# Gates made earlier in a two-layer PEER kernel, and four more places for its dense weight units

## The chip, the cores and the metric

One core of one Trainium2 chip runs the whole program in one launch. The metric is device time in microseconds (us). Three timed runs of the kernel before gave 2160.9, 2161.8 and 2163.95 us; the median is 2161.8 us. The profile is of one more execution.

## The reference, cut to what matters

256 tokens of 1024 features pass through two transformer layers (retention, then differential attention) and a third block (gated linear attention, MLA, cross attention, feed-forward). After each of the first two mixers stands a PEER feed-forward, and only it is touched by the change:

```python
def block(xc):                                    # 128 tokens
    q = (xc @ w_q).reshape(PEER_CHUNK, PEER_HEADS, 2, half)
    sc = jnp.einsum('thpd,hpnd->thpn', q, subkeys)            # 8 heads x 2 x 128 keys
    s1, i1 = lax.top_k(sc[:, :, 0], 16); s2, i2 = lax.top_k(sc[:, :, 1], 16)
    cand = s1[..., :, None] + s2[..., None, :]
    top, pos = lax.top_k(cand, 16)                            # 16 experts per head
    gate = jax.nn.softmax(top, axis=-1)
    u_e, v_e = jnp.take(u, idx, axis=0), jnp.take(v, idx, axis=0)   # of 16384 experts
    act = jax.nn.gelu(jnp.einsum('ted,td->te', u_e, xc))
    return jnp.einsum('te,ted->td', gate * act, v_e)
x = layer_norm(ALPHA * x + peer_ffn(x), g, b)
```

All of it is in float32.

## The kernel before, in words

The kernel splits the 256 tokens of each PEER layer in two.

**Dense tokens.** For the last 160 tokens (DENSE) all 16384 experts are computed. Both tables, u and v, are read once each as 128 units of 128 experts (512 KB per unit), by SyncE, in order, into N_PLAIN = 6 places (`plain`, in the room of the hi and lo weight splits, which idle in this stage). Unit i waits until TensorE has used unit i - 6. In the u stage TensorE takes two units per step c (c = 0 to 63, j = 0, 1), eight matmuls each (16 instructions in the profile), and ScalarE applies gelu. In the v stage (`second_weights`) it takes unit k = 0 to 127 against the gated activations `experts`. At k = 122 (128 - LATE) it waits until all looked-up experts are used (L1020), and after k = 127 turns the sums back to token order (`turn_back`).

**Looked-up tokens.** The first 96 tokens (LOOKED) use only their own 16 x 8 experts. With 128 partitions this makes 96 gathers (LISTS) of 128 rows of u, and 96 of v: q = 0 to 191, 512 KB each. GpSimd issues them (`look_up`, L3179) into six places (N_ROWS): gather q waits until VectorE has used row set q - 6. VectorE uses each in `look(q)` (L2495 for u, L2501 for v), at points of its own order of work that `peer_schedule` lays out: LOOKS_AT[c, j] in the u stage, LOOKS_AT[k] in the v stage. 90 looks fall in the u stage and 102 in the v stage.

**Gates.** VectorE finds the experts (`topk`) in pieces of YIELDS = 15 instructions between these points; they run out at c = 11. The softmax is ScalarE's Exp (before step c = LISTED = 20), VectorE's `gates` at c = 20 and TensorE's `turn` of three columns after the units of c = 20 (L819), then VectorE's `turned_gates` at c = 21. 20 looks stand ahead of `gates` on VectorE. On GpSimd (`beside_experts`) stand, in order: `early` = 26 gathers, four small DMAs of the lists, a wait for the gates, six small DMAs of the gates and a wait for their landing, then the builds. Before build i all gathers up to GATHERS[i] are issued: 29 before the first.

**Spread.** From step c = SPREAD = 22 on, the gates are placed into `experts` for four dense tokens at a time, 40 groups. GpSimd (L3168, two instructions), ScalarE and VectorE build one-hot rows for a group, TensorE multiplies them (`spread`, L967), ScalarE and VectorE place the result. There is one group for each c, and TensorE does spread(i - 1) where the others build i; its first is at c = 23, after the first unit.

**Later work in GpSimd's queue.** Between the gathers of q = 126 and 127 stands `later()`. In layer 0 it waits until TensorE has used v unit k = 48 and loads constants (L3253); in layer 1 it waits for k = 54 and loads the memory tokens and eight constants (L3272). In layer 1 VectorE and ScalarE also have steps of the third block between their looks (`remember`): at k = 72 to 84 angles and the norm of the memory tokens (L2740), which TensorE transposes at k = 90 and 92 (L819).

**End of a layer.** VectorE copies two of four v sums (`turned_back`, L2543), TensorE turns them, and VectorE adds them to x (L2184), takes statistics (L2189) and normalizes (`norm_steps`).

## Time and profile before

| | us |
|---|---|
| median of three runs | 2161.8 |
| profiled execution | 2162.51 |
| its span | 2160.6 |
| TensorE busy in it | 2011.0 |
| VectorE busy | 1384.3 |
| GpSimd busy | 659.0 |
| mean DMA rate over the span | 283 GB/s |

The profiled execution is 1.9 us longer than its span. A busy TensorE is not one at its peak: matmuls are pipelined. A stretch of the views is given in us from the start of the span, and "xN" counts instructions.

### The profile page before, as it was taken

How to read it: one execution, taken by the hardware profiler on the slowest of the kernel's cores; microseconds unless marked ns; L12 is line 12 of the kernel's file. 1: busy time of each engine (PE TensorE's matmuls, PEld its weight loads, DVE VectorE, ACT ScalarE, POOL GpSimd, SP SyncE). 2: the span in 40 equal slices, each digit the busy share in tenths (PEclk: the TensorE clock that was granted, in tenths of full speed). 3: DMA queues.
4: the chain of work that ended last, by engine and by line, in shares of the span. 5: the costliest groups of instructions: out<-in, count | busy, mean ns of one | idle time of the engine just before them, and what ended most of it. 6: DMA issues, size and time to landing. Idle time of an engine off the chain costs nothing.

```text
span 2160.6 us, 32850 instructions
## 1 busy us (share of the span) xinstructions
PE 2011.0 (93%) x13084; PEld 1842.1 (85%) x13084; DVE 1384.3 (64%) x2732; ACT 599.7 (28%) x1179; POOL 659.0 (31%) x631
## 2 busy tenths in 40 slices
PE   9999995899999998989999499999999499999999
PEld 9877995899998987867799499999998488777887
DVE  7567499677744344358759957774314725877885
ACT  3455411232200000026530023320000203665554
POOL 1000013888842333000101478884133510000000
PEclk9999998999999999989999799999999799999999
DMA  7546588999999999824558899999999993343665
GB/s 262 176 149 204 183 255 328 351 393 395 386 409 389 356 409 409 312 80 136 165 196 289 304 351 394 390 389 408 370 343 409 362 349 119 108 147 113 189 193 167
DMA packets 168952, 612.42 MB, mean 283 GB/s; under 512 B 19600, under 2 KB 19776, under 8 KB 168544
## 3 DMA queue, kind: packets, MB, share of 16 engines
q1 hardware_dynamic: 107712, 391.63, 50.4%
q0 software_dynamic: 60368, 217.38, 26.5%
q8 instruction: 105, 1.72, 0.3%
q10 hardware_dynamic: 720, 1.31, 0.2%
q14 instruction: 47, 0.39, 0.1%
HBM read 606.89 MB, written 1.05 MB: 281 GB/s over the span
## 4 chain that ended last, share of the span: by engine, by line
PE 64%; DMA 18%; DVE 14%; ACT 1%; issue 1%; POOL 1%; ACTq 0%; DVEq 0%; POOLq 0%
PE ps L981 18%; PE ps L1012 12%; DMA plain<-in_peer_v 12%; PE ps L684 5%; DMA big<-in_peer_v,big 4%; PE ps L720 4%; PE ps L723 4%; PE ps L727 3%; PE ps L767 3%; PE ps L687 3%; DVE big L2328 2%; PE ps L967 2%; DVE big L2096 2%; DVE big L2324 2%; PE ps L819 1%; PE ps L756 1%
## 5 line engine op out<-in xcount | busy, mean ns | idle before, releaser
L1012 PE MATMUL ps<-big,plain 128*128 128x160 f32 x4096 | 600.0, 305 | 29.5 <-DMA plain<-in_peer_v 20.3
L1012 PEld LDWEIGHTS ps<-big,plain 128*128 128x128 f32 x4096 | 568.1, 192 | 61.7 <-DMA plain<-in_peer_v 33.0
L981 PE MATMUL ps<-big,plain 128*128 128x160 f32 x4096 | 580.5, 302 | 1.0 <-DMA plain<-in_peer_u 0.8
L981 PEld LDWEIGHTS ps<-big,plain 128*128 128x128 f32 x4096 | 563.9, 191 | 1.9 <-issue 1.0
L2501 DVE SCALAR_TENSOR_TENSOR big<-big 128x1024 f32<-128x1024 f32 x188 | 241.5, 1284 | 311.6 <-DMA big<-in_peer_v,big 309.1
L2090 DVE TENSOR_TENSOR lo<-raw,hi 128x1024 fp32r<-128x1024 f32 (+1 forms) x195 | 236.2, 1219 | 102.8 <-ACT hi L1491 102.3
L3179 POOL DMA_INDIRECT big<-in_peer_v,big x192 | 192.1, 1001 | 278.4 <-DVE big L2501 255.1
L3179 POOL DMA_INDIRECT big<-in_peer_ur,big x192 | 221.2, 1152 | 145.6 <-DVE big L2495 91.6
L2495 DVE CUSTOM_DVE_ANT_0 big<-big 128x1024 f32<-128x1024 f32 x192 | 241.7, 1269 | 10.4 <-DMA big<-in_peer_ur,big 10.2
L1491 ACT ACTIVATE hi<-raw 128x1024 fp32r<-128x1024 f32 (+1 forms) x195 | 204.7, 1055 | 148.5 <-PE ps L727 53.0
L3168 POOL TENSOR_SCALAR lnp<-iota,selT 128x128 f32<-128x128 f32 x160 | 193.2, 1213 | 3.2
L1674 ACT ACTIVATE big<-ps 128x320 f32<-128x320 f32 (+39 forms) x126 | 44.4, 354 | 480.5 <-PE ps L981 453.9
L684 PE MATMUL ps<-xs,hi 128*128 128x512 f32 x512 | 128.8, 393 | 1.0 <-DVE big L3087 1.0
L819 PE MATMUL ps<-ident,big 128*128 128x128 f32 (+1 forms) x280 | 42.4, 285 | 86.0 <-DVE big L2462 54.4
L819 PEld LDWEIGHTS ps<-ident,big 128*128 128x128 f32 (+1 forms) x280 | 33.9, 144 | 95.6 <-DVE big L2462 55.4
L2441 DVE SCALAR_TENSOR_TENSOR big<-ps,big 128x192 f32<-128x192 f32 (+19 forms) x80 | 41.7, 521 | 109.2 <-ACT big L1666 88.1
L684 PEld LDWEIGHTS ps<-xs,hi 128*128 128x128 f32 x512 | 92.2, 189 | 17.8 <-DVE big L3087 1.1
L720 PE MATMUL ps<-hi,xs 128*128 128x512 f32 (+1 forms) x308 | 99.1, 403 | 1.9 <-ACT xs L1566 1.7
L723 PE MATMUL ps<-hi,xs 128*128 128x512 f32 (+1 forms) x308 | 95.7, 392 | 0.2 <-DVE xs L2216 0.2
L727 PE MATMUL ps<-lo,xs 128*128 128x512 f32 (+1 forms) x308 | 94.8, 389 | 0.5 <-DVE lo L2090 0.5
L1497 ACT ACTIVATE big<-ps 128x512 f32<-128x512 f32 (+6 forms) x121 | 64.8, 547 | 72.1 <-PE ps L727 46.7
L1491 ACT ACTIVATE tail_weights<-raw 128x1024 fp32r<-128x1024 f32 x3 | 3.2, 1058 | 270.5 <-PE ps L1012 270.5
(402 smaller groups left out, 2301.1 us busy)
## 6 DMA issues: line engine op xcount, KB each, us to landing
plain<-in_peer_u SPq DMA_DIRECT2D x256, 512.0 KB
plain<-in_peer_v SPq DMA_DIRECT2D x256, 512.0 KB
raw<-in_ret_vg SPq DMA_DIRECT2D x32, 512.0 KB
raw<-in_peer_q SPq DMA_DIRECT2D x24, 512.0 KB
raw<-in_ffn_up SPq DMA_DIRECT2D x22, 512.0 KB
raw<-in_ffn_down SPq DMA_DIRECT2D x22, 512.0 KB
raw<-in_ffn_gate SPq DMA_DIRECT2D x18, 512.0 KB
raw<-in_ret_qk SPq DMA_DIRECT2D x16, 512.0 KB
```

The lines of the kernel that those rows point to most:

```text
L684: e.matmul(out, uh[:, k, :], xs[:, k, :, :].rearrange("p h t -> p (h t)"), start=k == 0, stop=False)
L720: e.matmul(out, xh[:, 2 * s + i, cut], uh[:, i, :], start=s == 0 and i == 0, stop=False)
L723: e.matmul(out, xl[:, 2 * s + i, cut], uh[:, i, :], start=False, stop=False)
L727: ins = e.matmul(out, xh[:, 2 * s + i, cut], ul[:, i, :], start=False, stop=s == 3 and i == 1)
L981: ins = e.matmul(u.view[:, j * DENSE:(j + 1) * DENSE], w[:, k, :], Peer.xT[:, k, :], start=k == 0, stop=k == 7)
L1012: ins = e.matmul(us[b // 2].view[:, b % 2 * DENSE:(b % 2 + 1) * DENSE], w[:, b * 128:(b + 1) * 128], experts[:, k, :], start=k == 0 and b ...
L1491: e.activation(parts(i)[0][:, 0:w], raw[:, i % N_RAW, 0:w], ACT.Copy).then_inc(s_hi, 1)
L2090: e.tensor_tensor(ul[:, 0:w], raw[:, i % N_RAW, 0:w], uh[:, 0:w].bitcast(F32), ALU.subtract).then_inc(s_lo, 1)
L2495: e.tensor_tensor_reduce(rows, rows, copies, 1.0, 0.0, ALU.mult, ALU.add, w).then_inc(s_looked, 1)
L2501: e.scalar_tensor_tensor(out=sums, in0=rows, scalar=w, in1=sums, op0=ALU.mult, op1=ALU.add).then_inc(s_looked, 1)
L3168: ins = e.tensor_scalar(Peer.oha[i % 2][:, t % 4, :], iota[:, :], selT[:, 0, t:t + 1], selT[:, 2, t:t + 1], ALU.is_equal, ALU.mult)
L3179: e.indirect_dma_start(out=Peer.rows[m % N_ROWS], out_offset=None, in_=table, in_offset=bass.IndirectOffsetOnAxis(ap=Peer.idx[:, i:i + 1], ...
```

## The change

The gates follow the selection more closely: `gates` moves from c = 20 to c = 14 (GATED), the wait and the turn on TensorE from c = 20 to c = 23 (LISTED), `turned_gates` from c = 21 to c = 22 (TURNED), the first group from c = 22 to c = 26 (SPREAD), and the 40 groups then come five in nine units in place of one in two. From c = 12 to c = 25 VectorE has one look per c in place of four in five units, so that 9 looks stand ahead of `gates`, 15 gathers ahead of the gates' DMAs and 27 ahead of the first build on GpSimd; 82 looks fall in the u stage and 110 in the v stage. `later()` moves from behind q = 126 to behind q = 145.

The dense units get ten places: the four new ones lie in `xs`, the room of the hi and lo activations. In layer 0 all ten are used throughout; in layer 1 units from i = 210 (k = 82) on use only the first six, since `xs` is written again at k = 90. The first loads into the new places wait for the last matmul of the query projection.

At the end of a layer VectorE adds and takes statistics of the first half of the columns before it copies the last v sums.

```diff
-N_PLAIN, N_ROWS, LATE = 6, 6, 6
-YIELDS, LISTED, SPREAD, LOOKS = 15, 20, 22, 8
+N_PLAIN, N_FIRST, N_ROWS, LATE = 10, 6, 6, 6
+SLOTS = [[i % 10 for i in range(256)], [i % 10 if i < 210 else (i - 210) % 6 for i in range(256)]]
+YIELDS, GATED, TURNED, LISTED, SPREAD, LOOKS = 15, 14, 22, 23, 26, 8
...
-            n = 1 if c >= SPREAD and (2 * (c - SPREAD) + j) % 2 == 0 else 0
+            n = 1 if c >= SPREAD and (2 * (c - SPREAD) + j) % 9 % 2 == 0 else 0
...
-            n = 1 if c >= LOOKS and (2 * (c - LOOKS) + j) % 5 < 4 and q < LISTS else 0
+            n = 1 if c >= LOOKS and q < LISTS and ((2 * (c - LOOKS) + j) % 5 < 4 if c < GATED - 2 or c >= SPREAD else j == 0) else 0
...
+    later = min(q for k in range(58, 128) for q in looks[k]) + N_ROWS
...
-        plain = nc.alloc_sbuf_tensor_at("plain", [128, N_PLAIN, UNIT], F32, offset=split_at)
+        plain_a = nc.alloc_sbuf_tensor_at("plain", [128, N_FIRST, UNIT], F32, offset=split_at)
...
+        plain_b = nc.alloc_sbuf_tensor_at("plain_in_xs", [128, N_PLAIN - N_FIRST, UNIT], F32, offset=xs_at)
+        plain = [plain_a[:, i, :] for i in range(N_FIRST)] + [plain_b[:, i, :] for i in range(N_PLAIN - N_FIRST)]
...
-                    if c == LISTED - 1:
+                    if c == LISTED - 2:
                         for t in range(2):
                             e.wait_ge(s_sel, 2 * l + t + 1)
                             e.activation(Peer.sel[t][2], Peer.sel[t][2], ACT.Exp).then_inc(s_gexp, 1)
...
-                        if (c, j) == (LISTED, 0):
+                        if (c, j) == (GATED, 0):
                             gates()
-                        if (c, j) == (LISTED + 1, 0):
+                        if (c, j) == (TURNED, 0):
                             turned_gates()
...
-                for i in (0, 2):
-                    turned_back(l, i)
+                turned_back(l, 0)
+                for t in range(2):
+                    residual(f"peer_v{l}", t, 0)
+                for t in range(2):
+                    stats(f"peer_v{l}", t, 0)
+                turned_back(l, 2)
...
-                early = N_ROWS + sum(len(LOOKS_AT[c, j]) for c in range(LISTED) for j in range(2))
+                early = N_ROWS + sum(len(LOOKS_AT[c, j]) for c in range(GATED) for j in range(2))
...
-                    if q == LISTS + 30:
+                    if q == LATER:
                         later()
...
             def plain_load(l, i):
                 if i < N_PLAIN:
-                    e.wait_ge(s_used, split_before[m] + 1)
+                    e.wait_ge(s_used, split_before[l, i] + 1)
                 else:
-                    e.wait_ge(*plain_used(l, i - N_PLAIN + 1))
+                    e.wait_ge(*plain_used(l, max(n for n in range(i) if SLOTS[l][n] == SLOTS[l][i]) + 1))
```

`residual` is the addition to x (L2184) and `stats` the statistics (L2189) of one half, cut out of `norm_steps`, which leaves out the first half for these two stages.

## Rows read from the trace of the kernel before

**Rows 1.** The page's busy times, whole span: engine, us, share, instructions.
```profile
PE 2011.0 (93%) x13084; PEld 1842.1 (85%) x13084; DVE 1384.3 (64%) x2732; ACT 599.7 (28%) x1179; POOL 659.0 (31%) x631
```

**Rows 2.** Waits of TensorE, 240 to 960: us in total, times, longest.
```profile
PE ps L819 <- DVE big L2462: 26.9, 1, 26.9
PE ps L819 <- DVE x L2201: 4.0, 1, 4.0
```

**Rows 3.** Waits of TensorE, 1100 to 1830.
```profile
PE ps L819 <- DVE big L2740: 29.2, 1, 29.2
PE ps L819 <- DVE big L2462: 27.5, 1, 27.5
```

**Rows 4.** Windows: length, busy us of PE, PEld, DVE, ACT, POOL; PEclk; DMA share; GB/s.
```profile
630.00:675.00 45.00, 42.94 (x283) 38.59 (x282) 22.23 (x18) 0.00 (x0) 16.81 (x18) 1.00 1.03 409
680.00:712.00 32.00, 31.53 (x225) 30.57 (x226) 6.42 (x5) 0.00 (x0) 0.00 (x0) 1.00 0.91 320
1125.00:1150.00 25.00, 25.00 (x186) 25.00 (x186) 24.80 (x168) 2.62 (x6) 0.00 (x0) 1.00 0.75 244
1540.00:1590.00 50.00, 49.49 (x361) 48.76 (x360) 4.70 (x4) 0.00 (x0) 6.89 (x11) 1.00 0.88 296
```

**Rows 5.** Timeline of VectorE, 360 to 383: start, us, what [idle before <-releaser].
```profile
360.29 1.22 DVE L2495 CUSTOM_DVE_ANT_0 big<-big 128x1024 f32<-128x1024 f32 x1
369.77 1.22 DVE L2495 CUSTOM_DVE_ANT_0 big<-big 128x1024 f32<-128x1024 f32 x1 [1.38 <-DMA big<-in_peer_ur,big]
380.87 0.28 DVE L2107 TENSOR_REDUCE sm<-big 128x8 f32<-128x128 f32 x1
382.18 0.29 DVE L2462 TENSOR_TENSOR big<-big,sm 128x128 f32<-128x128 f32 x1
```

**Rows 6.** Timeline of TensorE at the gates' turn and the first group, layer 0.
```profile
381.77 1.66 PE L819 MATMUL ps<-ident,big 128*128 128x128 f32 x6 [26.87 <-DVE big L2462]
398.36 0.62 PE L967 MATMUL ps<-lnp 128*128 128x128 f16 x8 [2.23 <-issue]
```

**Rows 7.** Timeline of GpSimd, 363 to 417, layer 0.
```profile
363.77 1.99 POOL L3179 DMA_INDIRECT big<-in_peer_ur,big  x1 [0.30 <-issue]
366.06 1.99 POOL L3179 DMA_INDIRECT big<-in_peer_ur,big  x1 [0.30 <-issue]
383.00 2.08 POOL L3193 DMA_DIRECT2D big<-big  x4
392.27 1.83 POOL L3179 DMA_INDIRECT big<-in_peer_ur,big  x1 [4.20 <-issue]
396.67 1.59 POOL L3168 TENSOR_SCALAR lnp<-iota,selT 128x128 f32<-128x128 f32 x2
413.10 3.90 POOL L3168 TENSOR_SCALAR lnp<-iota,selT 128x128 f32<-128x128 f32 x2
```

**Rows 8.** Groups on GpSimd, 405 to 585: busy us, mean ns, idle before.
```profile
L3168 POOL TENSOR_SCALAR lnp<-iota,selT 128x128 f32<-128x128 f32 x76 | 94.9, 1254 | 1.5
L3179 POOL DMA_INDIRECT big<-in_peer_ur,big x59 | 68.3, 1157 | 17.0 <-issue 12.1 <-DVE big L2495 4.9
```

**Rows 9.** Timeline of GpSimd at `later()`, layers 0 and 1.
```profile
712.45 0.58 POOL L3253 DMA_DIRECT2D big<-in_c_diff_cs  x1 [34.85 <-PE ps L1012]
1581.48 0.77 POOL L3272 DMA_DIRECT2D big<-in_mem  x1 [47.10 <-PE ps L1012]
```

**Rows 10.** Timeline of VectorE and TensorE, v stage of layer 0: start, last look, k = 122.
```profile
595.06 28.44 PE L1012 MATMUL ps<-big,plain 128*128 128x160 f32 x208
887.98 1.28 DVE L2501 SCALAR_TENSOR_TENSOR big<-big 128x1024 f32<-128x1024 f32 x1 [1.28 <-DMA big<-in_peer_v,big]
900.73 3.60 PE L1024 MATMUL ps<-big,selT 128*128 128x512 f32 x8
```

**Rows 11.** v stage of layer 1: its start in the chain, k = 122 in the timeline.
```profile
1452.12 34.93 PE ps L1012 x256
1779.06 3.60 PE L1024 MATMUL ps<-big,selT 128*128 128x512 f32 x8
```

More of the change, by code:

```diff
@@ L240, in peer_schedule @@
     assert q == 2 * LISTS and last is not None
-    return steps, looks, tokens, gathers, last
-STEPS_AT, LOOKS_AT, TOKENS, GATHERS, ALL_LOOKED = peer_schedule()
+    later = min(q for k in range(58, 128) for q in looks[k]) + N_ROWS
+    return steps, looks, tokens, gathers, last, later
+STEPS_AT, LOOKS_AT, TOKENS, GATHERS, ALL_LOOKED, LATER = peer_schedule()
 def build(nc, A, OUT):
@@ L631, in build @@
             for i in range(N_PLAIN):
-                m = 256 * l + i
-                split_before[m] = max(n for n in in_ring[m % N_PLAIN % N_SPLIT] if n < end)
+                split_before[l, i] = max(n for n in in_ring[i % N_SPLIT] if n < end) if i < N_FIRST else end - 1
             for r in range(N_SPLIT):
                 n = min(n for n in in_ring[r] if n >= end)
-                m = max(m for m in range(256 * l, 256 * l + 256) if m % N_PLAIN % N_SPLIT == r)
-                W.after[n] = (*W.after.get(n, ()), (s_pused, m + 1))
+                i = max(i for i in range(256) if SLOTS[l][i] in (r, r + N_SPLIT))
+                W.after[n] = (*W.after.get(n, ()), (s_pused, 256 * l + i + 1))
         n = W.first["diff_k0"]
@@ L2176, in acc, with residual, stats @@
                         left(k + lead)
+            def residual(stage, t, h):
+                u, xp = use[stage, 2 * t + h], x[:, t, h * 512:(h + 1) * 512]
+                e.wait_ge(*u.filled)
+                e.scalar_tensor_tensor(out=xp, in0=xp, scalar=ALPHA, in1=u.view, op0=ALU.mult,
+                                       op1=ALU.add).then_inc(u.freed[0], 1)
+            def stats(stage, t, h):
+                e.wait_ge(*use[stage, 2 * t + h].freed)
+                me.did(e.bn_stats(st[:, (2 * t + h) * 6:(2 * t + h + 1) * 6], x[:, t, h * 512:(h + 1) * 512]))
             def norm_steps(i, stage, tiles=(0, 1)):
+                halves_left = (1,) if stage in ("peer_v0", "peer_v1") else (0, 1)
                 for t in tiles:
                     xt = x[:, t, :]
-                    for h in range(2):
-                        u, xp = use[stage, 2 * t + h], x[:, t, h * 512:(h + 1) * 512]
-                        e.wait_ge(*u.filled)
-                        e.scalar_tensor_tensor(out=xp, in0=xp, scalar=ALPHA, in1=u.view, op0=ALU.mult,
-                                               op1=ALU.add).then_inc(u.freed[0], 1)
+                    for h in halves_left:
+                        residual(stage, t, h)
                     yield
-                    for h in range(2):
-                        e.wait_ge(*use[stage, 2 * t + h].freed)
-                        me.did(e.bn_stats(st[:, (2 * t + h) * 6:(2 * t + h + 1) * 6], x[:, t, h * 512:(h + 1) * 512]))
+                    for h in halves_left:
+                        stats(stage, t, h)
                     me.wait()
```

22 lines of the change are left out of this document (11 added, 11 removed).

## The prediction

> **What bounds the kernel now.** I read the page's busy times, the waits of TensorE, windows of 25 us and shorter, and then the timelines of the engines in turn where TensorE stood still. TensorE is busy for 2011.0 of 2160.6 us [rows 1], so most of the kernel is paced by it. The reader is to see three other things.
>
> First, three long waits: 26.9 and 27.5 us for the gates at the turn (L819 for L2462), once a layer, and 29.2 us in layer 1 for the normed memory tokens (L2740) [rows 2, 3].
>
> Second, which bound holds between the waits. An undisturbed TensorE takes 186 instructions in 25 us, so a dense unit of 16 costs 25 x 16 / 186 = 2.15 us, and that needs 0.524 MB / 2.15 us = 244 GB/s [rows 4]. With gathers beside it the DMA engines stand at 409 GB/s, or 1.28 us for a transfer of 512 KB, and TensorE takes 283 instructions in 45 us: 2.54 us per unit, twice the 1.28 us. The two streams then share evenly; I count 2.56 us for a unit and 2.56 us for a gather, side by side. So the v stages are DMA-bound while gathers remain, and TensorE-bound afterwards.
>
> Third, the gathers stop in each v stage for `later()`, which waits 34.85 and 47.10 us for TensorE [rows 9]. In these stretches the DMA engines move 320 and 296 GB/s in place of 409 [rows 4]. In layer 1 the stop also delays VectorE's looks, and with them the memory tokens' norm that stands between them: the 29.2 us of [rows 3].
>
> **The gates (layer 0; layer 1 alike).** TensorE stops at 381.77 - 26.87 = 354.9 [rows 6] with the 42 units of c = 0 to 20 done. The change lets it go on to the end of c = 23, 6 x 2.15 = 12.9 us, until 367.8. The selection ends just before the look at 360.29 [rows 5], as now, since YIELDS is the same. Three looks of 1.22 us and the gates (380.87 to 382.47, 1.6 us) put the gates at 360.3 + 3.7 + 1.6 = 365.6, 2 us before TensorE asks. That wait goes.
>
> What is late next is the first group. GpSimd's fifteenth gather is the one at 366.06, done at 368.05 [rows 7]. Behind it stand the ten small DMAs and their landing, 383.00 to 392.27 = 9.3 us, so gathers resume at 377.3. Then 12 gathers precede the first build, where 3 do now, and the last of them waits for the look of the first six. Gather to look took 369.77 - 363.77 = 6.0 us [rows 5, 7]. So: first of the twelve landed at 383.5; two more at 2.56 us each beside the dense stream; then TensorE stands, the ten places fill, and three come at 1.28 us, the sixth by about 392.5. Look 1.2, the gather it releases 1.1, a build 1.6 [rows 7]: the first group's rows are there at 396.4, and TensorE can start at about 397. It asks at 367.8 + 1.7 for the turn + 7 units x 2.15 = 384.5. A wait of some 12.5 us takes the place of 26.9. Now the first group is at 398.36 with 47 units done [rows 6]; then it is at about 397 with 55. Gain 8 x 2.15 + 1.4 = 18.6 us. Bounds: no wait at the group, 26.9 + 2.2 = 29 us; all twelve spaced by 2.56 us and a look between, TensorE at 405, gain 17.2 - 6.6 = 10.6 us. I take 18.6, since the places do fill once TensorE stands.
>
> **The denser groups.** In nine units TensorE needs 9 x 2.15 + 5 x 0.56 = 22.2 us (the turn of a group is L967, 0.62 us with its start [rows 6]). GpSimd needs 5 builds of (94.9 + 1.5) / 38 = 2.54 us and 7.2 gathers of (68.3 + 12.1) / 59 = 1.36 us [rows 8]: 22.5 us. It becomes the bound by 0.3 us in nine units, 3 us over 76; now it has 4.5 x 2.54 + 9.8 = 21.2 us of work in 21.9 us. A u stage gains 18.6 - 3 = 15.6 us. ScalarE and VectorE have room (VectorE 64% busy over the span [rows 1]).
>
> The Trainium skill (SBUF — State Buffer, "Who interferes with whom") says that a VectorE instruction with two SBUF inputs blocks GpSimd instructions that read SBUF, fully. The trace shows build pairs from 1.59 to 3.90 us [rows 7]; what makes the slow ones no row here shows. If denser work on VectorE did this more often, that is the slower rival below.
>
> **The v stages.** Layer 0 runs from 595.06 to k = 122 at 900.73, its last look ends at 889.3 [rows 10]. Check of the two-stream count: 102 looks x 2.56 = 261 us, plus 35 us of stop, is 296; it took 294. TensorE gets 259 / 2.56 = 101 units in it, 35 / 2.15 = 16 more in the stop, less 3 raw weight units in the same queue: 114.5. It had in fact used 122 - 11.4 / 2.15 = 116.7 when the looks ended, so it entered the stage with a lead of 2.2 units.
>
> After the change 110 looks remain, 110 x 2.56 - 2 = 280 us, with no stop if `later()` comes after k = 48: at q = 145, 58 looks or 148 us into the stage, TensorE is at k = 58 or more, and needs 48 (54 in layer 1). Four more places are a lead of up to 4 more units, filled while DMA has room (244 of 409 GB/s before the gathers start [rows 4]). TensorE then has used 280 / 2.56 - 3 + 6.2 = 112.6 units when the looks end, and reaches k = 122 after 280 + 9.4 x 2.15 = 300 us, against 305.7. Gain 5.7 us in layer 0. If the four places give nothing, 8.6 us less.
>
> Layer 1 now takes 1779.06 - 1452.12 = 327 us [rows 11]. After the change the same 280 us apply, plus 11 us for the constants, 4.3 transfers of 512 KB in the gathers' half (now in the stop, where DMA has room). In 291 us TensorE uses 291 / 2.56 - 3 + 6.2 = 116.9 units, then 5.1 x 2.15: 302 us. Gain 25 us. The memory tokens stay a wait of perhaps 10 us at k = 90 and 92, since the look of k = 84 (the 84th in the stage) ends at 84 x 2.56 + 11 for the constants = 226 us, the norm is a few us behind it, and TensorE can be at k = 92 by (92 - 6) x 2.56 = 220. It is free: the transfers go on behind it, and TensorE catches up before the looks end. From k = 82 on six places do as well as ten, because the dense stream has none landed ahead of use.
>
> **The end of a layer.** One addition and one statistic of 512 columns (0.65 us each, by half of 1.28 us for a look's 1024 columns [rows 10]) leave the path behind the last sums; they move under the last 12 half units on TensorE. TensorE's 4.0 us for the norm [rows 2] shrink by 1.3 us in layer 0; in layer 1 other matmuls cover it. The same work costs 2.7 us if it delays the last copies; the last units cover it. The second tile's share is hidden. Everything else (another ring order behind the stage, first loads of the new places) I put at 0, within 1 us either way.
>
> **Sum.** Layer 0: 15.6 + 5.7 + 1.3 = 22.6. Layer 1: 15.6 + 25 = 40.6. Together 63 us. The profiled execution took 2162.5 us, 0.7 us above the median of the runs, so the forecast is 2162.5 - 63 = 2099 us.
>
> **The rivals.**
> - *No wait at the first group.* The gathers land before 384.5, and 12.5 us more are saved in each layer: 2099 - 25 = 2074 us. For it: a gather alone is issued each 1.25 us. Against it: 12 of them behind a resumption at 377.3 with a latency of 6 us.
> - *The four places give nothing.* The lead is spent before the v stage because GpSimd's gathers take the DMA share: 2 x 8.6 = 17 us less, 2116 us. For it: the lead of 2.2 units out of six places now. This is the case in which half of the change doesn't do what it says.
> - *TensorE still waits long for the memory tokens or the stop stays.* The 110 later looks outweigh the stop removed, and 20 to 24 of layer 1's 25 us are not won: 2122 us. For it: the norm stands behind the 84th look of the stage, and 8 more looks are in it. Against it: the stop of 47 us goes.
> - *GpSimd becomes the bound: slower.* A pair of builds took from 1.59 to 3.90 us [rows 7], mean 2.50. Were all 3.90 in the denser order, 40 groups x 1.4 = 56 us are lost per layer in the u stage, 2099 + 112 = 2211 us. It decides for slower once a group costs 5.3 us in place of 4.5 (63 / 80 = 0.8 us more). Against it: VectorE's work per group hardly changes, only its spacing by a tenth.
>
> **How the numbers follow.** Chances: forecast 0.54, no wait 0.12, places give nothing 0.20, memory wait 0.09, slower 0.05. The lower end is the second case, 2074. At the upper end I add to the forecast the bound of the first group (8 us per layer) and half of the places' worth: 2099 + 16 + 9 = 2124, which holds the two middling cases. 0.2% or 4.3 us is about what can be told from no change; hardly any case ends there. Faster 0.93, same 0.02, slower 0.05.
>
> **What would show it.** Right: TensorE's wait for L2462 under 3 us; its wait before the first L967 near 12 us, and the first group at 397 in layer 0 with 55 units done; u stages ending 14 to 17 us earlier; no GpSimd wait of over 5 us at L3253 and L3272; L2740 under 15 us; 409 GB/s through the v stages until the looks end. Wrong: builds on GpSimd above 3 us a pair, a DMA-starved u stage, or a v stage of layer 0 that is not shorter than 305 us.

## The result

The kernel after takes 2132.6 us, median of four runs (2125.96 to 2137.1); the kernel before ran in 2162.9 us beside it (2160.9 to 2164.7, four runs). The ratio is 0.9858, 95% interval [0.9829, 0.9886]. Forecast were 2099 us and 63 us of gain; measured are 30, and the time lies outside the range, which ended at 2124. The profiled execution took 2137.1 us with a span of 2135.3 us; it is the slowest of the four, which matters for the stretch of the first group below.

### The waits that went and the ones that came

The page's busy times of the kernel after, against [rows 1]:

```profile
PE 2012.5 (94%) x13084; PEld 1841.6 (86%) x13084; DVE 1381.9 (65%) x2724; ACT 601.8 (28%) x1171; POOL 652.2 (31%) x631
```

Waits of TensorE in the kernel after, 240 to 960 and then 1100 to 1830 (us in total, times, longest), against [rows 2] and [rows 3]:

```profile
PE ps L972 <- POOL lnp L3185: 23.0, 1, 23.0
PE ps L972 <- issue: 4.9, 5, 1.6
PE ps L824 <- DVE x L2214: 3.6, 1, 3.6
...
PE ps L972 <- POOL lnp L3185: 21.9, 1, 21.9
PE ps L972 <- issue: 5.4, 3, 2.5
PE ps L985 <- DMA plain<-in_peer_u: 3.8, 1, 3.8
PE ps L824 <- DVE big L2757: 3.6, 1, 3.6
```

L985 and L1016 are the units of the u and v stage, L972 the groups' `spread`, L824 the turns. The waits for the gates are gone in both layers, the one for the memory tokens' norm fell from 29.2 to 3.6 us. In their place TensorE waits 23.0 and 21.9 us for the first group, some 5 us per layer for later ones, and 3.8 us for the first unit of layer 1.

### The first group

Timelines of VectorE, TensorE and GpSimd in the kernel after (start, us, what [idle before <-releaser]), against [rows 5 to 7]:

```profile
365.31 0.30 DVE L2475 TENSOR_TENSOR big<-big,sm 128x128 f32<-128x128 f32 x1
389.32 1.23 DVE L2508 CUSTOM_DVE_ANT_0 big<-big 128x1024 f32<-128x1024 f32 x1 [11.02 <-DMA big<-in_peer_ur,big]
...
367.28 0.82 PE L824 MATMUL ps<-ident,big 128*128 128x128 f32 x6
406.36 1.01 PE L972 MATMUL ps<-lnp 128*128 128x128 f16 x8 [23.04 <-POOL lnp L3185]
407.17 4.57 PE L985 MATMUL ps<-big,plain 128*128 128x160 f32 x16
...
365.29 0.94 POOL L3196 DMA_INDIRECT big<-in_peer_ur,big  x1 [0.30 <-issue]
366.23 2.08 POOL L3210 DMA_DIRECT2D big<-big  x4
380.99 0.99 POOL L3196 DMA_INDIRECT big<-in_peer_ur,big  x1 [9.70 <-issue]
402.75 0.94 POOL L3196 DMA_INDIRECT big<-in_peer_ur,big  x1 [0.30 <-issue]
403.74 2.51 POOL L3185 TENSOR_SCALAR lnp<-iota,selT 128x128 f32<-128x128 f32 x2
```

The gates end at 365.6 us and TensorE turns them at 367.28 without a wait, both as forecast. Then each step of GpSimd is later than forecast: the small DMAs land so that the gathers resume at 380.99 (forecast 377.3), the first of the twelve reaches its look after 8.3 us in place of 6.0 (389.32 - 380.99), and the twelfth is issued at 402.75. The first group's matmuls start at 406.36 (forecast 397). In four kernels of the experiments (gates_only, places6, later_old and order, called the four unchanged kernels below) GpSimd's and VectorE's order of work in this stretch is that of the kernel after; there the matmuls start at 403.1 to 404.6 us, and the profiled execution of the kernel after is 2 to 3 us later than these.

GpSimd's groups of instructions, 405 to 594 us (busy us, mean ns | idle before), against [rows 8]:

```profile
L3185 POOL TENSOR_SCALAR lnp<-iota,selT 128x128 f32<-128x128 f32 x80 | 96.7, 1213 | 1.5
L3196 POOL DMA_INDIRECT big<-in_peer_ur,big x60 | 70.8, 1179 | 20.9 <-issue 10.9 <-DVE big L2508 10.0
```

That is 80 x 1.213 = 97 us of builds and 60 gathers that with the gap of issue ahead of them take (70.8 + 10.9) / 60 = 1.36 us, 82 us: 179 of 189 us, and the other 10 us are waits for VectorE's looks, which wait for gathers. GpSimd is full. It nearly was before: [rows 8] hold 176.8 of 180 us and 4.9 us of such waits. This is the row on which the experiments below turn.

The Trainium skill (SBUF — State Buffer, "Who interferes with whom") speaks of VectorE's two-input instructions blocking GpSimd; the prediction let this stand as a cause of the slow rival. A build instruction takes 1213 ns after and took 1254 before [rows 8], so the denser order did not bring more of it; whether it occurs at all no row here shows.

### The v stages

Windows of the kernel after (columns as in [rows 4]), and timelines at `later()`, at the first and last look and at k = 122, against [rows 9 to 11]:

```profile
680.00:712.00 32.00, 30.60 (x204) 27.70 (x203) 16.10 (x13) 0.00 (x0) 12.48 (x13) 1.00 1.03 409
1540.00:1590.00 50.00, 47.61 (x316) 43.11 (x315) 24.55 (x21) 0.00 (x0) 19.62 (x20) 1.00 1.03 409
...
745.83 0.60 POOL L3270 DMA_DIRECT2D big<-in_c_diff_cs  x1
1600.06 0.78 POOL L3289 DMA_DIRECT2D big<-in_mem  x1
...
593.98 4.51 PE L1016 MATMUL ps<-big,plain_in_xs 128*128 128x160 f32 x32
880.55 1.28 DVE L2514 SCALAR_TENSOR_TENSOR big<-big 128x1024 f32<-128x1024 f32 x1 [1.25 <-DMA big<-in_peer_v,big]
898.07 3.60 PE L1028 MATMUL ps<-big,selT 128*128 128x512 f32 x8
...
1448.36 4.51 PE L1016 MATMUL ps<-big,plain_in_xs 128*128 128x160 f32 x32
1753.59 3.60 PE L1028 MATMUL ps<-big,selT 128*128 128x512 f32 x8
```

No stop is left at `later()` and the DMA engines stay at 409 GB/s, as forecast. The v stage of layer 0 takes 304.1 us up to k = 122 (305.7 before), that of layer 1 305.2 (327). The end of layer 0 is 1.1 us shorter: TensorE's wait for the norm is 3.6 us against 4.0, and the wait right behind it (L725) 2.1 against 2.7.

### The profile page after: what moved, and what is told of

It reads as the page before. It is cut to its first block, busy times and chain, and to the rows that moved or that the text cites. A ratio compares the mean times of both kernels' runs of the same rounds, so it can differ in the third digit from the quotient of the medians.

```text
span 2135.3 us, 32826 instructions
## 1 busy us (share of the span) xinstructions
PE 2012.5 (94%) x13084; PEld 1841.6 (86%) x13084; DVE 1381.9 (65%) x2724; ACT 601.8 (28%) x1171; POOL 652.2 (31%) x631
## 4 chain that ended last, share of the span: by engine, by line
PE 47%; DMA 22%; DVE 9%; issue 2%; POOL 2%; ACT 1%; ACTq 0%; DVEq 0%
PE ps L985 15%; DMA plain<-in_peer_v 11%; DMA big<-in_peer_v,big 8%; PE ps L1016 8%; PE ps L689 4%; PE ps L772 3%; PE ps L725 2%; PE ps L728 2%; PE ps L692 2%; PE ps L732 2%; PE ps L972 2%; PE ps L761 2%; DMA big<-in_peer_ur,big 1%; DVE big L2341 1%; PE ps L824 1%
## 5 line engine op out<-in xcount | busy, mean ns | idle before, releaser
L1016 PE MATMUL ps<-big,plain 128*128 128x160 f32 x2752 | 406.1, 305 | 17.1 <-DMA plain<-in_peer_v 12.9
L1016 PEld LDWEIGHTS ps<-big,plain 128*128 128x128 f32 x2752 | 383.5, 193 | 39.1 <-DMA plain<-in_peer_v 20.9
L985 PE MATMUL ps<-big,plain 128*128 128x160 f32 x2496 | 358.4, 303 | 3.8 <-DMA plain<-in_peer_u 3.8
L985 PEld LDWEIGHTS ps<-big,plain 128*128 128x128 f32 x2496 | 346.8, 192 | 4.0 <-issue 4.0
L3196 POOL DMA_INDIRECT big<-in_peer_v,big x192 | 186.3, 970 | 325.0 <-DVE big L2514 296.2
L2508 DVE CUSTOM_DVE_ANT_0 big<-big 128x1024 f32<-128x1024 f32 x192 | 234.9, 1241 | 60.5 <-DMA big<-in_peer_ur,big 60.4
L985 PE MATMUL ps<-big,plain_in_xs 128*128 128x160 f32 x1600 | 227.6, 300 | 0.0
L985 PEld LDWEIGHTS ps<-big,plain_in_xs 128*128 128x128 f32 x1600 | 219.5, 190 | 0.0
L1016 PE MATMUL ps<-big,plain_in_xs 128*128 128x160 f32 x1344 | 197.4, 303 | 14.5 <-DMA plain_in_xs<-in_peer_v 11.7
L1016 PEld LDWEIGHTS ps<-big,plain_in_xs 128*128 128x128 f32 x1344 | 184.4, 190 | 26.6 <-issue 14.7
L1678 ACT ACTIVATE big<-ps 128x320 f32<-128x320 f32 (+35 forms) x126 | 45.6, 362 | 436.1 <-PE ps L985 436.1
L972 PE MATMUL ps<-lnp 128*128 128x128 f16 x640 | 50.8, 221 | 55.2 <-POOL lnp L3185 44.9
L725 PE MATMUL ps<-hi,xs 128*128 128x512 f32 (+1 forms) x308 | 99.1, 403 | 1.6 <-ACT xs L1570 1.4
```

The costliest lines, as they stand in the source:

```text
L725: e.matmul(out, xh[:, 2 * s + i, cut], uh[:, i, :], start=s == 0 and i == 0, stop=False)
L985: ins = e.matmul(u.view[:, j * DENSE:(j + 1) * DENSE], w[:, k, :], Peer.xT[:, k, :], start=k == 0, stop=k == 7)
L1016: ins = e.matmul(us[b // 2].view[:, b % 2 * DENSE:(b % 2 + 1) * DENSE], w[:, b * 128:(b + 1) * 128], experts[:, k, :], start=k == 0 and b ...
L2508: e.tensor_tensor_reduce(rows, rows, copies, 1.0, 0.0, ALU.mult, ALU.add, w).then_inc(s_looked, 1)
L3196: e.indirect_dma_start(out=Peer.rows[m % N_ROWS], out_offset=None, in_=table, in_offset=bass.IndirectOffsetOnAxis(ap=Peer.idx[:, i:i + 1], ...
```

## The experiments

The table holds the medians of four to six runs each, and lengths from the profiled execution: a u stage from its first unit to the first unit of the v stage, a v stage from there to k = 122. The kernel before ran in 2161.9 to 2163.2 us beside them.

| kernel | us | ratio [95%] | u 0 | v 0 | u 1 | v 1 | first group, layer 0 |
|---|---|---|---|---|---|---|---|
| before | 2162.9 | 1 | 336.2 | 305.7 | 339.1 | 327.1 | 398.4 |
| after | 2132.6 | 0.9858 [0.9829, 0.9886] | 334.6 | 304.1 | 335.1 | 305.2 | 406.4 |
| b_later | 2148.8 | 0.9933 [0.9921, 0.9946] | 337.8 | 309.6 | 338.2 | 309.1 | 399.1 |
| gates_only | 2150.3 | 0.9945 [0.9929, 0.9960] | 331.8 | 309.2 | 331.6 | 320.4 | 403.3 |
| places6 | 2145.2 | 0.9917 [0.9905, 0.9930] | 330.7 | 312.2 | 333.2 | 313.7 | 403.2 |
| later_old | 2132.9 | 0.9867 [0.9853, 0.9882] | 331.7 | 302.1 | 331.8 | 309.6 | 403.1 |
| ramp | 2136.4 | 0.9873 [0.9852, 0.9895] | 334.3 | 303.6 | 336.1 | 305.1 | 399.5 |
| waits | 2124.0 | 0.9830 [0.9814, 0.9847] | 328.5 | 303.9 | 330.2 | 303.8 | 400.8 |
| order | 2123.3 | 0.9825 [0.9809, 0.9841] | 331.2 | 303.9 | 331.3 | 305.3 | 404.6 |
| all3 | 2112.8 | 0.9774 [0.9761, 0.9788] | 322.3 | 303.3 | 322.8 | 304.4 | 394.2 |
| few | 2104.3 | 0.9733 [0.9711, 0.9756] | 319.1 | 305.1 | 318.3 | 303.8 | 383.3 |
| few58 | 2106.4 | 0.9745 [0.9726, 0.9765] | 314.5 | 306.5 | 318.2 | 310.4 | 383.2 |
| ramp_half | 2112.6 | 0.9776 [0.9758, 0.9793] | 325.3 | 303.2 | 324.5 | 303.8 | 399.3 |
| few_half | 2083.1 | 0.9631 [0.9615, 0.9647] | 305.1 | 307.1 | 304.5 | 309.0 | 382.7 |
| after_dve | 2116.3 | 0.9786 [0.9767, 0.9805] | 325.6 | 303.4 | 325.4 | 303.2 | 402.9 |
| few_dve | 2082.5 | 0.9626 [0.9610, 0.9641] | 306.6 | 307.0 | 306.7 | 307.8 | 383.5 |

### Fewer gathers ahead of the first build (ramp)

```diff
-            gathers += [q + N_ROWS] * len(steps[c, j])
+            gathers += [q + min(N_ROWS, len(gathers))] * len(steps[c, j])
```

> Twenty-one gathers stand ahead of the first build of a u stage instead of 27 (the lead of the gathers over the builds grows to six over the first groups instead of starting there). In the changed kernel the last twelve gathers ahead of the first build take 380.99 to 402.75 us, 1.8 us each. Theory A (TensorE's wait for the first group is what is paid, and TensorE sets the pace behind it): the first build starts about 6 x 1.8 = 10.9 us earlier, TensorE's wait falls from 23.0 to about 12 us in each layer, the v stage starts 11 us earlier, and the kernel takes about 2111 us (ratio 0.976 to the kernel before). Theory B (GpSimd is itself the bound between the first group and the v stage: 60 gathers of 1.48 us with their gap and 80 builds of 1.21 us are 186 of the 187.6 us there): the wait for the first group falls as in A, but the waits for later groups grow by as much, the v stage starts within 2 us of where it did, and the time is 2129 to 2133 us (0.985).

TensorE's waits for groups in ramp (us in total, times, longest), and its first group:

```profile
PE ps L972 <- DVE lnp L2445: 37.5, 5, 16.9
PE ps L972 <- issue: 11.2, 8, 1.6
...
399.50 1.01 PE L972 MATMUL ps<-lnp 128*128 128x128 f16 x8 [16.92 <-DVE lnp L2445]
...
393.94 5.10 POOL L3185 TENSOR_SCALAR lnp<-iota,selT 128x128 f32<-128x128 f32 x2 [6.56 <-DVE negT L2491]
```

The first group came 3.6 us earlier than in the earliest of the four unchanged kernels, 6.9 us earlier than in the profiled kernel after (399.5 us; its wait is now for VectorE's part, not GpSimd's), and nothing was left of it at the v stage: the u stages take 334.3 and 336.1 us, as in the profiled kernel after and 2.5 to 4.8 us more than in the four unchanged kernels. The waits went as theory B said; the time, 2136.4 us, is 3 us above its range. The third line shows why GpSimd won nothing: it waited 6.56 us for VectorE ahead of its first build, where in the kernel after it waited as long in all for looks among the last twelve gathers (2.59, 1.40 and 2.39 us). An earlier first group is worth nothing as long as GpSimd's own queue ends no sooner; that it is this queue which counts, ramp_half below shows.

### The wait for the small DMAs moved (waits)

```diff
-                e.wait_ge(s_list, 96 * (l + 1))
-                e.wait_ge(s_lgate, 96 * (l + 1))
...
+                    if i == 0:
+                        e.wait_ge(s_list, 96 * (l + 1))
+                        e.wait_ge(s_lgate, 96 * (l + 1))
                     build(l, i)
```

> GpSimd's wait for the small transfers of the list and the gates stands right ahead of the first build instead of ahead of the last twelve gathers. Theory A (those 9.7 us of wait are what made the first group come at 406 and not at 397 us): gathers resume at about 371.3 us instead of 381.0, the first build starts at about 394 us, TensorE's wait for it falls from 23.0 to about 13.5 us, and since GpSimd's whole work starts earlier the v stage starts 9 us earlier in each layer: about 2114 us (0.977). Rival: the gathers were held by VectorE's looks, which free their places (it ended 6.4 us of idle time of GpSimd among these twelve gathers), so that the looks and not the wait set the first build: it starts within 3 us of 403.7, and the time is 2127 to 2132 us (0.985).

GpSimd in waits, timeline:

```profile
371.53 1.00 POOL L3196 DMA_INDIRECT big<-in_peer_ur,big  x1 [0.30 <-DVE big L2508]
383.93 0.93 POOL L3196 DMA_INDIRECT big<-in_peer_ur,big  x1 [3.74 <-DVE big L2508]
397.71 3.02 POOL L3185 TENSOR_SCALAR lnp<-iota,selT 128x128 f32<-128x128 f32 x2
```

The gathers resume at 371.53, 9.5 us earlier. But six of them fill the places, and from 383.93 on all but the last wait for a look that waits for a gather: the first build starts at 397.7, 6 us earlier than in the kernel after. Against the four unchanged kernels the first group is 2.3 to 3.8 us earlier and the u stages are 1.1 to 3.3 us shorter. The whole kernel gains 8.7 us against the median of the kernel after; the stages show about half of that, and the two ratio intervals overlap (up to 0.9847 here, from 0.9829 there). Neither theory's number is met: what the wait no longer takes, the looks take in part, 3.74 us at the first of them.

### Layer 1's order of places (order)

```diff
-SLOTS = [[i % 10 for i in range(256)], [i % 10 if i < 210 else (i - 210) % 6 for i in range(256)]]
+FIRST = [4, 5, 0, 1, 2, 3, 6, 7, 8, 9]
+SLOTS = [[i % 10 for i in range(256)], [FIRST[i % 10 if i < 210 else (i - 210) % 6] for i in range(256)]]
...
-                split_before[l, i] = max(n for n in in_ring[i % N_SPLIT] if n < end) if i < N_FIRST else end - 1
+                split_before[l, i] = max(n for n in in_ring[SLOTS[l][i] % N_SPLIT] if n < end) if i < N_FIRST else end - 1
```

> Layer 1 takes its places in the order 4, 5, 0, 1, 2, 3, 6 to 9 instead of 0 to 9. Theory A (TensorE's 3.8 us wait for a dense unit at 1113.25 us, with 4.6 us over it at the lower clock, comes of the place's split form, which the last units of layer 0 free late): the wait is gone, the first key scores of layer 1 end 5 to 6 us earlier, about 2127 us (0.983). Rival (the unit's transfer is late for another reason, the ring of transfers at the turn of the layer): the wait stays at 3 to 4 us, and the time is that of the changed kernel, 2133 us (0.986).

TensorE at the first unit of layer 1, in the kernel after and in order:

```profile
1113.25 4.61 PE L985 MATMUL ps<-big,plain 128*128 128x160 f32 x16 [3.79 <-DMA plain<-in_peer_u]
```

```profile
1105.53 2.34 PE L986 MATMUL ps<-big,plain 128*128 128x160 f32 x16
```

The wait is gone, and with it the slow first unit (4.61 us for 16 instructions; 2.34 in order) behind it. From k = 122 of layer 0 to the first unit of layer 1 it takes 210.4 us in place of 215.2. Theory A is right: the wait is the order's. The two profiles put its cost at 4.8 + 2.3 = 7 us; between the medians lie 9.3 us, but the ratio intervals overlap (up to 0.9841 here, from 0.9829 in the kernel after), so that some 7 us is the surer number. The wait is also there in places6, later_old and gates_only (3.6 to 3.9 us), which all begin layer 1 with place 0, and not in the kernel before, which begins it with place 4.

### The three together (all3)

> The three edits together: 21 gathers ahead of the first build, the wait for the small transfers behind them, and layer 1's places in the order of the kernel before. If all three are paid at TensorE: first build at about 384 us (six gathers of 1.3 us from 371.3, then the looks' pace), TensorE's wait for the first group 3 us or none, 20 us per layer and 6 for the order: about 2087 us (0.965). If GpSimd bounds the stretch behind the first group, only its earlier start counts, 9 us per layer, and the order's 6: about 2108 us (0.975).

2112.75 us, 5 us above the second number and 26 above the first: the second theory. Here the ramp does pay: against waits the u stages are 6.2 and 7.4 us shorter, where against the kernel after it gained nothing: GpSimd here goes on with its gathers from 371.09 us, as in waits, and no longer has six of them to wait for ahead of its first build. TensorE now waits 11.4 and 12.2 us for VectorE's part of the first group.

### Fewer looks ahead of the first group (few)

```diff
-... ((2 * (c - LOOKS) + j) % 5 < 4 if c < GATED - 2 or c >= SPREAD else j == 0) else 0
+... ((2 * (c - LOOKS) + j) % 5 < 4 or c >= 46 if c < GATED - 2 or c >= SPREAD else j == 0 and c % 2 == 0) else 0
```

> The kernel with the three edits (all3, 2112.75 us), and one more: between the gates and the first group VectorE has one look for two steps c, six in place of twelve, and 14 gathers stand ahead of the first build in place of 21; the six looks are made up behind step 46. Theory A (the remaining wait for the first group, 11.4 and 12.2 us, is set by VectorE, whose part of the group stands behind twelve looks that each wait for a gather, 2.5 us apart): the first group comes at about 383 us in place of 394, the wait falls under 3 us, and as GpSimd's queue is shorter too the v stage starts 8 to 11 us earlier: about 2093 us (0.968). Theory B (GpSimd's sum of gathers and builds, 82 - 14 + 6 gathers and 80 builds, is the bound as it was with the gathers' lead alone): the groups behind it wait instead, gain under 3 us: 2110 to 2113 us (0.977).

```profile
383.34 0.62 PE L973 MATMUL ps<-lnp 128*128 128x128 f16 x8
...
PE ps L973 <- issue: 19.5, 14, 3.4
PE ps L973 <- DVE lnp L2446: 3.4, 4, 1.6
```

Above: TensorE's first group in few, then its waits for groups. The first group comes at 383.34 with no wait at all, 23 us earlier than in the kernel after. Of the 11 to 12 us won there, 3.2 and 4.5 us arrive at the v stage; the waits for later groups rose from 8.0 (all3) to 19.5 us in both layers together, and 3.4 us of waits for VectorE's part came with them. The time, 8.4 us less than all3, lies between the theories' numbers (under 3 us, and 20) and nearer B's: most of what was won at the first group was given back behind it.

### GpSimd's work halved (ramp_half, few_half)

```diff
-                for t in (t0, t0 + 1):
+                for t in (t0,) if i >= 2 else (t0, t0 + 1):
                     ins = e.tensor_scalar(Peer.oha[i % 2][:, t % 4, :], iota[:, :], ...
```

> The kernel with 21 gathers ahead of the first build (ramp, 2136.4 us), in which GpSimd from the third group on makes one of its two rows and leaves the other out, so that 38 instructions of 1.21 us per layer, 46 us, are missing from its queue. Theory B (GpSimd's sum bounds the stretch from the first group to the v stage, and took back the 7 us that the first group came earlier): the first group stays at about 399.5 us, the waits for later groups go, and the v stage starts 5 to 8 us earlier in each layer: 2121 to 2126 us (0.982). Rival (VectorE's looks or TensorE itself took them back): v stage start within 2 us, 2132 to 2137 us (0.987).

> The kernel with one look for two steps c ahead of the first group (few, 2104.3 us), with one of GpSimd's two rows left out from the third group on, 46 us less per layer in its queue. Theory B (the 11 to 12 us per layer that TensorE there waits for groups are GpSimd's): they go to under 3 us, v stage 8 to 9 us earlier per layer, 2086 to 2089 us (0.965). Rival (the waits are for ScalarE's or VectorE's part of a group): at most 4 us in all, 2100 to 2105 us (0.973).

In ramp_half the first group is where it was in ramp (399.3 us), and the u stages are 9.0 and 11.6 us shorter; in few_half 14.0 and 13.8 us. Behind the first five groups no wait of TensorE for a group is longer than 0.7 us. So GpSimd's sum is what took back the gain of ramp and few: shown, by the one edit that touches nothing else. Both gains are larger than expected (23.8 us where 10 to 15 were, 21.3 where 15 to 18 were): the u stages fell by some 5 and 8 us more than the waits for groups that the profile names. The granted clock accounts for most of that. Windows from the first group to the v stage, layer 0, in few and few_half (columns as in [rows 4]):

```profile
383.34:578.71 195.37, 184.23 (x1491) 181.00 (x1489) 144.88 (x289) 57.33 (x187) 173.66 (x146) 0.98 0.99 381
```

```profile
382.74:564.12 181.38, 179.81 (x1491) 177.81 (x1489) 142.80 (x289) 57.11 (x187) 138.32 (x108) 1.00 1.02 406
```

TensorE does the same 1491 instructions and is busy 4.4 us less (in layer 1 3.2 us, 182.64 and 179.42), with its clock at 1.00 in place of 0.98: with the waits go the slow instructions behind them, 7.6 us in both layers. From ramp to ramp_half it is 3.8 us (367.4 and 363.6 us busy in both layers).

### The row moved to VectorE (after_dve, few_dve)

```diff
-                for t in (t0, t0 + 1):                       # GpSimd
+                for t in (t0,):
...
-                    e.tensor_scalar(rows[:, 2, :], iota[:, :], selT[:, 0, t:t + 1], selT[:, 2, t:t + 1], ALU.is_equal,
-                                    ALU.mult)                # VectorE
+                    for r in (1, 2):
+                        e.tensor_scalar(rows[:, r, :], iota[:, :], selT[:, 0, t + r - 2:t + r - 1],
+                                        selT[:, 2, t + r - 2:t + r - 1], ALU.is_equal, ALU.mult)
```

> The changed kernel, with one of GpSimd's two rows of a group made by VectorE (0.41 us there for the like row, 40 a layer, 16 us; GpSimd loses 1.2 us a group, 48 us). Nothing is left out. Theory B (in the changed kernel GpSimd's sum behind the first group costs the waits for later groups, 5 us a layer, while the first group's time is set by the gathers ahead of it): the first group stays at 402 to 406 us, the later waits go, the v stages start 5 us earlier: about 2122 us (0.981). Rival (VectorE, which stands 33 us for ScalarE's part in this stretch, is the next bound, so that the row only moves the wait): 2130 to 2136 us (0.986).

> The kernel few (2104.3 us), with one of GpSimd's two rows of a group made by VectorE; nothing is left out. Theory B (the waits for groups are GpSimd's, and VectorE has room for 16 us in a stretch in which it is busy 133 of 178 us): near the kernel with the rows left out, 2083.05 us, plus 2 to 4 us for VectorE's part: 2085 to 2089 us (0.965). Rival (VectorE becomes late for the looks, whose rows then come free later, and the groups wait for it): 2098 us or more (0.971).

Waits of TensorE in after_dve, and GpSimd's groups of instructions there, 405 to 590 us:

```profile
PE ps L972 <- POOL lnp L3186: 39.9, 2, 20.1
...
L3197 POOL DMA_INDIRECT big<-in_peer_ur,big x61 | 74.4, 1220 | 64.0 <-DVE big L2509 56.3 <-issue 7.7
L3186 POOL TENSOR_SCALAR lnp<-iota,selT 128x128 f32<-128x128 f32 x39 | 42.8, 1097 | 4.6 <-PE ps L972 3.0
```

In the changed kernel as it stands, the first group stays at 402.9 us with its 20 us of wait, all later waits for groups are gone, and the u stages take 325.6 and 325.4 us: 5 to 8 us less than in the four unchanged kernels. GpSimd's idle time before gathers rises from 10.0 us to 56.3 us: it has room again. The time is 16.3 us lower, more than the 10 expected.

few_dve computes all and takes 2082.5 us, as little as the kernel with the row left out (2083.1, the intervals overlap): 80 us less than the kernel before and 50 less than the kernel after. VectorE takes 0.36 us for such a row (mean of 160 in few_dve) where GpSimd takes 1.2.

### Places and later() (places6, later_old, gates_only, b_later)

```diff
places6:    -N_PLAIN = 10, SLOTS with i % 10        +N_PLAIN = 6, SLOTS with i % 6
later_old:  -if q == LATER:                         +if q == LISTS + 30:
gates_only: both of these
b_later:    (kernel before) -if q == LISTS + 30:    +if q == 153:
```

> The changed kernel with six places for the dense units in place of ten, all else the same (layer 1 then starts at place 4, as in the kernel before). Theory A (the prediction's: four places are a lead of four units at the v stage, 8.6 us per layer): the v stages are 8 to 9 us longer than 304.1 and 305.2 us; but the wait at layer 1's first unit, 3.8 us and some 5 us more behind it, goes too: 2132.6 + 17 - 8.5 = 2141 us (0.990). Rival (the places give nothing, TensorE waits for groups anyway and the lead is spent): 2133 - 8.5 = 2124 us (0.982).

The expectation is wrong in one point: layer 1 starts at place 0 in places6, and its wait of 3.7 us stayed. The v stages are 8.1 and 8.5 us longer than in the kernel after: the 8.6 us per layer of the prediction. The median is 12.6 us higher.

> The changed kernel with later() back between the gathers 126 and 127. At that place 38 looks of the v stage are done where 30 were in the kernel before, and TensorE stands 4 units further ahead, so that the wait for unit 48 should be about 10 us and the one for unit 54 about 21 us (34.9 and 47.1 before). Theory A (a stop costs what the DMA engines leave unused in it, 0.22 to 0.28 of its length): 2 us in layer 0 and 6 us in layer 1, 2141 us (0.990). Theory B (the stop costs above all by the wait for the memory tokens' norm, which came back with it): that wait is 15 us or more and the time above 2145 us. Rival (the stop was hidden): 2131 to 2134 us.

> The kernel before with one edit: later() stands between the gathers 152 and 153, where TensorE has used unit 54. Theory A (of the 25.5 us that layer 1's v stage and its start gained, the stop's removal made most): no GpSimd wait of over 5 us at the loads, TensorE's wait for the memory tokens' norm falls from 29.2 to under 10 us, layer 1's v stage takes 312 us in place of 327 and layer 0's 299 in place of 305.7: about 2141 us (0.990). Rival (the four places made it): the v stages stay within 4 us of 305.7 and 327, and the time within 6 us of 2162 us.

> The changed kernel with six places for the dense units and with later() back behind q = 126: what is left of the change is the move of the gates, the groups and the looks, and the end of a layer. Theory A (the stop at later() shrinks by itself, since eight more looks stand in the v stage and q = 126 comes 8 looks later in it): the stop is 13 and 27 us in place of 35 and 47, and moving later() back costs no more than in the changed kernel with ten places: 2143 to 2147 us (0.992). Theory B (with six places the stop's removal is worth what it was to the kernel before alone, 13.7 us): 2156 to 2160 us (0.998).

GpSimd at `later()` in later_old (two lines, layers 0 and 1), gates_only (two) and, without a wait, b_later:

```profile
700.79 0.59 POOL L3270 DMA_DIRECT2D big<-in_c_diff_cs  x1 [6.32 <-PE ps L1016]
1562.80 0.77 POOL L3289 DMA_DIRECT2D big<-in_mem  x1 [20.17 <-PE ps L1016]
```

```profile
711.68 0.58 POOL L3269 DMA_DIRECT2D big<-in_c_diff_cs  x1 [16.86 <-PE ps L1015]
1579.88 0.77 POOL L3288 DMA_DIRECT2D big<-in_mem  x1 [30.86 <-PE ps L1015]
```

```profile
749.21 0.60 POOL L3253 DMA_DIRECT2D big<-in_c_diff_cs  x1
```

The stop shrank by itself from 35 and 47 us to 17 and 31 with six places and to 6 and 20 with ten, since eight more looks stand in the v stage. Between gates_only, places6, later_old and the kernel after the medians are 2150.3, 2145.2, 2132.9 and 2132.6 us: ten places are worth 17.4 or 12.6 us, moving `later()` 5.1 or 0.3 us. So later_old came out as its rival said (2131 to 2134 us: the stop is hidden), with layer 1's v stage 4.4 us longer and layer 0's 2.0 us shorter; gates_only lies between its two ranges, 3 us above A's. To the kernel before alone the move is worth 14 us (b_later), all of it in layer 1: its v stage fell by 18.0 us, while that of layer 0 *grew* by 3.9 where 6.7 us less were expected. In each pair of kernels that differ by `later()` alone, layer 0's v stage is longer without the stop: 309.6 against 305.7, 312.2 against 309.2, 304.1 against 302.1.

Why it grows can be read from the last look: in b_later it ends at 863.47 + 1.28 = 864.8, 42 us ahead of k = 122 at 907.08, where TensorE has the DMA engines to itself and does not fill them. The stretch from the last look to k = 122 in b_later and in the kernel before (columns as in [rows 4]):

```profile
864.80:907.00 42.20, 42.20 (x313) 42.20 (x312) 2.32 (x2) 1.06 (x1) 0.00 (x0) 1.00 0.72 252
```

```profile
889.30:900.70 11.40, 11.40 (x86) 11.40 (x85) 2.23 (x2) 0.00 (x0) 0.00 (x0) 1.00 0.84 291
```

In the kernel before this tail was 900.73 - 889.3 = 11.4 us [rows 10]. A stop lets TensorE run ahead and ends the looks later; without it idle DMA time comes at the end. Counted as the share of 409 GB/s left unused, it is 16 us in b_later's tail, and 8 us in the stop (320 GB/s, [rows 4]) with 3 us in the tail of the kernel before: an estimate from these rows that gives 5 us for the measured 3.9. In layer 1 the stop did cost, because the memory tokens' norm stood behind it.

### Looks made up later (few58)

> The kernel few, in which the looks are made up only behind step 58 and not behind 46: 77 looks in place of 82 in the u stage, 115 in the v stage. Theory (the look-outs for groups at 493 to 548 us come of gathers and builds of GpSimd beside looks at every half step; a look moved to the v stage costs 2.56 - 2.15 = 0.41 us there): group waits fall from 11 to some 4 us per layer, the v stages grow by 2 us each: 2 x (7 - 2) = 10 us less, 2094 us (0.969). Rival (the bound is elsewhere, or the v stage pays 2.5 us for a look): 2104 us or more (0.973).

Missed: 2106.4 us, the same as few. Layer 0's u stage lost 4.6 us, but layer 1's v stage gained 6.6: with 115 looks in it, TensorE at k = 122 waits 3.2 us for the last look. There the looks, not TensorE, end last, so that a further one should cost its full 2.56 us (not run). In layer 1 the u stage did not get shorter at all (318.3 and 318.2 us).

## Why the prediction was wrong, step by step

Two steps failed on the way to "a u stage gains 15.6 us", and one small term: the wait of 12.5 us for the first group, which is 19 to 23 us; the 3 us for GpSimd as a bound, which are 5.6 us in the changed kernel and 12 where the first group has no wait at all (few); and the order of the places, put at 0 and worth some 7 us.

| term | forecast | measured | how |
|---|---|---|---|
| u stage, layer 0 | 15.6 | 4.5 | 336.2 - 331.7, median of the kernel after and the four unchanged kernels |
| v stage, layer 0 | 5.7 | 1.6 | 305.7 - 304.1 |
| end of layer 0 | 1.3 | 1.1 | profile after |
| turn to layer 1 | 0 | -3.8 | the new wait at L985 |
| u stage, layer 1 | 15.6 | 7.3 | 339.1 - 331.8, as above |
| v stage, layer 1 | 25 | 21.9 | 327.1 - 305.2 |
| sum | 63 | 33 | between medians 30.3 |

**The gates** come at 365.6 us as forecast, the turn at 367.28 (367.8), and the wait is gone: right.

**"A wait of some 12.5 us takes the place of 26.9"**: wrong by 6 to 9 us in time of the first group, and the wait is 23.0 us (19.3 to 20.7 in the four unchanged kernels). Three sizes were taken from stretches in which TensorE stood still or had just begun again: the landing of the small DMAs (3.7 us later here), the latency of a gather (6.0 us; 8.3 here) and the pace of twelve gathers. With the gates' wait removed TensorE and its loads run beside the first two. The prediction's own upper bound, 405 us, was the right value. By place, this is the larger part of what the u stages missed: of the 11 us of layer 0, 6 to 8 stand here. after_dve, where GpSimd has room, keeps the first group at 402.9 us and its u stages, 325.6 and 325.4 us, are still 5.0 and 1.9 us above the forecast ones. But correcting this step alone would not have saved the forecast: ramp had the first group at 399.5 us and lost it all behind it.

**"It becomes the bound by 0.3 us in nine units, 3 us over 76"**: this is the step that failed in kind, and not in size only. The count of GpSimd's work was right (22.5 us in nine units of 22.2 us; 179 of 189 us found, and 10 of waits for looks), and it was set against TensorE's 22.2 us as a small surcharge. But a bound is not a surcharge on a gain made elsewhere: from the first build to the v stage GpSimd has about 180 us of work, and 10 us of waits for looks, and a u stage can end earlier only by as much as GpSimd *starts* earlier or works less. Its first build moved from 396.67 [rows 7] to 403.74, the wrong way, and six gathers fewer stand behind it, 6 x 1.36 = 8.2 us: together 1.1 us earlier, and the v stage starts at 593.98 in place of 595.06. I counted eight units done before the first group as 8 x 2.15 us of gain, though the groups behind it had then to come in less time, from an engine that had none to spare. From the first group to the v stage after_dve takes 181.9 and 181.3 us, the kernel after 187.6 and 186.8: 5.6 us per layer are this bound's in the changed kernel, where the forecast had 3. With the first group's wait gone too (few against few_dve) it is 12. The two failed steps don't add: the first group's lateness hid about half of the second.

**"Gain 5.7 us in layer 0"**: the places gave their 8.1 (8.6 forecast), eight more looks cost 2.6 (places6 against b_later; 8 x 0.41 = 3.3 by the count), but the stop's removal cost 3.9, where the prediction's count had it as a gain of about 0.4 (5.7 - 8.6 + 3.3). Sum 1.6.

**"Gain 25 us" in layer 1**: 18.0 for the stop and the norm's wait (b_later), 8.5 for the places, -4.6 for the looks: 21.9. The norm's wait fell to 3.6 us, further than the 10 forecast.

**"Everything else ... I put at 0, within 1 us"**: the order of the places cost some 7 us (3.8 of wait, 2.3 of a slow unit in the profiled execution). It was in the diff (layer 1 begins with place 0 in place of 4), it was named and put at nothing, without asking which load has to wait for the last weights in that room.

**The rivals**: "the places give nothing" is refuted. "GpSimd becomes the bound" was named, but tied to a slower kernel by way of slow builds; in its plain form, full with builds of the usual length, it needed no change of any row. It could not make the kernel slower, only keep the gain away.

What remains open: the part of the 8.7 us between waits and the kernel after that the stage lengths don't show, why ramp's u stages are longer than those of the four unchanged kernels, and why a build or a gather on GpSimd varies between 0.9 and 2 us.

## What to carry to other kernels

Before a wait is counted as gained, add up the work of each engine from the new release point to the end of the stage; the stage can't end before the engine with the largest sum, and a nearly full one (here GpSimd, 21.2 us in 21.9 before) gives back most of what is won ahead of it. When two streams share the DMA engines and one of them ends first, a pause in that one can be free, as the 35 us of layer 0 were here, and what counts is the tail in which the other runs alone. Durations of small transfers are taken from a stretch that is as busy as the new one.

## What the runs showed of the hardware

The landing of small transfers under load. DMA issues (KB each, median us to landing) in the kernel before, 380 to 395 us, just after TensorE stood still for 27 us (280 GB/s in the window), and in the kernel after, 364 to 376 us, beside units and gathers (337 GB/s):

```profile
big<-big POOLq DMA_DIRECT2D x8, 4.0 KB, 4.3
```

```profile
big<-big POOLq DMA_DIRECT2D x8, 4.0 KB, 8.6
```

A transfer of 4 KB took 4.3 us in the one and 8.6 in the other (medians of eight); GpSimd's wait rose with it from 4.2 to 9.7 us. The Trainium skill (DMA: Bandwidth & Descriptors, "Latency and other measured facts") has the latency of an access to HBM rise with the load, from 0.2 us on average to 2 us. These transfers go from SBUF to SBUF, for which it has no such figure; were it the same, at most 1.8 us would have been added (an estimate from that page's figures), not the 4.3 measured.

A wait of TensorE can cost more than its length. After 23 us of standing the first unit took 4.57 us for its 16 instructions, against 2.34 us, half the speed, as at the lower of the clock's two levels (1.2 and 2.4 GHz); the mean granted clock of the window around it is 0.77 (columns as in [rows 4]):

```profile
400.00:425.00 25.00, 18.64 (x136) 18.56 (x137) 14.26 (x30) 5.45 (x17) 21.12 (x19) 0.77 0.81 264
```

After 3.8 us of standing at the start of layer 1 the first unit took 4.61 us in the kernel after and in ramp, but 2.41 to 3.38 us in six others. Where the wait was gone (2.34 us in few and order), so was the slow unit. Why it varies after so short a stand no row here shows.
